# Expert routing of token pairs inside the output-projection stage, first expert block fixed and fetched early, residual written twice

## The reference, cut to what matters

```
mix = concat(groups) @ w_out
h   = LayerNorm(alpha * x + mix)
g_logits = h @ w_router_group + b          # 4 groups; the group with the largest logit is taken
e_logits = h @ w_router_expert + b         # 8 experts in that group; the top 2 are taken
gate = softmax(g_logits)[group] * softmax(top 2 logits)
moe  = sum over the 2 experts of gate * ((silu(h @ w1[e]) * (h @ w3[e])) @ w2[e])
out  = LayerNorm(alpha * h + moe)
```

## Time and profile before

| what | us |
|---|---|
| median of 3 runs (lowest, highest) | 2583.19 (2578.44, 2587.91) |
| the profiled execution, own time | 2585.68 |
| its span, first to last instruction | 2583.8 |
| third stage, from its first transfer to its last DVE instruction | 1304.89 to 1575.20 |
| fourth stage, to its last DVE instruction | to 1630.80 |
| first expert product | 1653.15 |
| fetches of expert weights (L1713), 2 MB each | 96 |

### The profile page before, as it was taken

The page is one execution under the profiler, slowest core; times in us unless marked ns, Lnnn a source line. Parts: engine busy times, 40 slices in busy tenths (PEclk is TensorE's granted clock), DMA queues, the critical chain, the costliest instruction groups (busy, mean ns, idle before and its releaser), DMA issues. The chain is left out here.

```text
span 2583.8 us, 42394 instructions
## 1 busy us (share of the span) xinstructions
PE 2292.1 (89%) x13288; PEld 1857.2 (72%) x13289; DVE 1595.6 (62%) x2749; ACT 1203.5 (47%) x1969; POOL 310.9 (12%) x223
## 2 busy tenths in 40 slices
PE   5999999897999999999959993599999999999950
PEld 5989998796666666666747882487877788888840
DVE  4444454555776767767745446577886765656538
ACT  4233334333665666656632220356765645446423
POOL 0000000000000000000001110013233322222315
PEclk9999999998999999999979996799999999999975
DMA  4001001121000000000043324599999978877825
GB/s 169 26 25 41 24 24 48 63 74 32 5 6 6 10 12 10 12 6 9 7 143 114 114 89 161 203 335 339 362 352 323 336 228 279 294 243 260 261 76 241
DMA packets 151085, 346.41 MB, mean 134 GB/s; under 512 B 25024, under 2 KB 37056, under 8 KB 150720
## 3 DMA queue, kind: packets, MB, share of 16 engines
q1 hardware_dynamic: 137888, 297.48, 31.7%
q0 software_dynamic: 13104, 47.72, 7.5%
HBM read 296.41 MB, written 57.67 MB: 137 GB/s over the span
## 5 line engine op out<-in xcount | busy, mean ns | idle before, releaser
L1862 DVE TENSOR_TENSOR w_raw<-w_raw,w_hi 128x4096 f32 (+1 forms) x96 | 424.2, 4419 | 142.0 <-ACT w_hi L1853 141.5
L1853 ACT CAST w_hi<-w_raw 128x4096 fp32r (+1 forms) x96 | 347.2, 3633 | 119.7 <-DMA w_raw<-in_w 109.0
L1802 PE MATMUL eH<-w_hi,xh 128*128 128x512 f32 x720 | 290.5, 404 | 15.5 <-DVE xl L1920 15.5
L1803 PE MATMUL eH<-w_hi,xl 128*128 128x512 f32 x720 | 286.7, 398 | 0.0
L943 PE MATMUL pS<-kT,qT 128*128 128x512 f32 (+3 forms) x640 | 260.2, 533 | 4.8 <-ACT pr L1032 4.4
L1040 ACT CAST prT_hi<-pT 128x512 fp32r<-128x512 f32 (+1 forms) x288 | 162.5, 564 | 197.9 <-PE pT L953 197.5
L1118 DVE TENSOR_TENSOR prT_lo<-pT,prT_hi 128x512 fp32r<-128x512 f32 (+1 forms) x288 | 189.4, 659 | 94.3 <-ACT prT_hi L1040 93.8
L1109 DVE TENSOR_REDUCE mx<-pS 128x1 f32<-128x512 f32 (+2 forms) x320 | 191.5, 608 | 15.3 <-PE pS L943 9.0
L1807 PE MATMUL eH<-w_raw,xh 128*128 x720 | 184.4, 398 | 5.5 <-DVE w_raw L1862 5.5
L943 PEld LDWEIGHTS pS<-kT,qT 128*128 128x128 f32 x640 | 111.2, 190 | 106.7 <-issue 61.9
L1802 PEld LDWEIGHTS eH<-w_hi,xh 128*128 128x128 f32 x720 | 136.6, 190 | 47.9 <-issue 15.3
(11 more groups left out here) (324 smaller groups left out, 4980.4 us busy)
## 6 DMA issues: line engine op xcount, KB each, us to landing
w_raw<-in_w SPq DMA_DIRECT2D x96, 2048.0 KB
xt<-in_x SPq DMA_DIRECT2D x16, 1024.0 KB, 5.0
xs<-in_x SPq DMA_DIRECT2D x8, 1024.0 KB, 5.0
scratch_h<-hp SPq DMA_DIRECT2D x16, 512.0 KB, 2.9
fz<-scratch_z SPq DMA_DIRECT2D x16, 512.0 KB, 10.8
out<-fz SPq DMA_DIRECT2D x16, 512.0 KB, 2.6
scratch_rT<-ot SPq DMA_DIRECT2D x8, 512.0 KB, 2.9
scratch_a<-a_out SPq DMA_DIRECT2D x64, 64.0 KB, 1.7
```

The source lines that it names most:

```text
L1802: pe.matmul(H[:], xh[:, k, :], w.hi[:, k, :], start=(k == 0), stop=False)
L1803: pe.matmul(H[:], xl[:, k, :], w.hi[:, k, :], start=False, stop=False)
L1853: nc.scalar.copy(w.hi[:], w.words(o).bitcast(F32)).then_inc(w.hi_ready, 1)
L1862: v.tensor_tensor(w.words(o), w.words(o).bitcast(F32), w.hi[:].bitcast(F32), ALU.subtract).then_inc(w.lo_ready, 1)
```

## The change

The picking of group and experts, the ranks and the one-hot rows for a pair of tiles are done in the third stage, two steps later: step m (from m = 2) does tiles 2(m - 2) and 2(m - 2) + 1. `choose` (21 DVE instructions, each waiting for the one before) stands behind `invert(m + 1)` and ahead of tile 0's L1423; one copy of the ranks stands behind tile 1's `split_r`; `ranked` and `spots` (14 instructions) stand at the end of the step, ahead of the next step's `split_a`. PE gets two small products ahead of tile 1's logits. Only the last four tiles are left for the fourth stage. A running count per expert (`carry`) replaces the scan over all tiles. Expert 0 always gets at least one block, so that block 0 belongs to expert 0 and its weights are fetched in the fourth stage without knowing the routing, with block 0's rows gathered there too. SP stores each tile of `h` a second time to `z` and the copy of `h` to `z` goes. The 32 products for tokens are separate from 32 products for gates, and block 0's rows depend on the first only. Router weights and constants are loaded in the third stage. In the fifth stage DVE splits block 0's rows before it splits w1.

```diff
+LATE = 4
+EARLY = (NT - LATE) // 2
+CHOOSE, PLACE = 21, 13
...
+def choose(v, go, t, s, pair, w):
...
+    go(v.tensor_tensor(t["gexp"][:, pair, :], G, bc(s["gmax"][:], NG), ALU.subtract))
+    go(v.tensor_tensor(s["geq"][:], G, bc(s["gmax"][:], NG), ALU.is_equal))
+    go(v.scalar_tensor_tensor(s["geq"][:], s["geq"][:], -64.0, row(R_LATE, NG), ALU.mult, ALU.add))
+    go(v.tensor_reduce(s["ix"][:], s["geq"][:], AX, ALU.min))
+
+    go(v.tensor_tensor(s["eq"][:], row(R_GROUP, NE), bc(s["ix"][:], NE), ALU.is_equal))
+    go(v.tensor_scalar(s["eq"][:], s["eq"][:], BIG, -BIG / 2, ALU.mult, ALU.add))
+    go(v.tensor_tensor(s["e1"][:], E, s["eq"][:], ALU.min))
+    for k, (src, m) in enumerate(((s["e1"], s["m1"]), (s["e2"], s["m2"]))):
+        go(v.tensor_reduce(m[:], src[:], AX, ALU.max))
+        go(v.tensor_tensor(s["eq"][:], src[:], bc(m[:], NE), ALU.is_equal))
+        go(v.scalar_tensor_tensor(s["eq"][:], s["eq"][:], -64.0, row(R_LATE, NE), ALU.mult, ALU.add))
+        go(v.tensor_reduce(s["ix"][:], s["eq"][:], AX, ALU.min))
+        go(v.tensor_tensor(t["oh"][:, k, pair, :], row(R_EXPERT, NE), bc(s["ix"][:], NE), ALU.is_equal))
+        if k == 0:
+            go(v.scalar_tensor_tensor(s["e2"][:], t["oh"][:, 0, pair, :], -BIG, s["e1"][:], ALU.mult, ALU.add))
+    go(v.tensor_tensor(s["both"][:], t["oh"][:, 0, pair, :], t["oh"][:, 1, pair, :], ALU.add))
+    go(v.tensor_tensor(t["de"][:, pair], s["m2"][:], s["m1"][:], ALU.subtract))
+
+
...
+    for i in range(w):
+        go(v.tensor_tensor(s["rk"][:, i], ranks[:, 0, i], t["carry"][:], ALU.add))
+        go(v.tensor_tensor(t["carry"][:], ranks[:, 1, i], t["carry"][:], ALU.add))
+
+
+def spots(v, go, t, s, pair, w):
...
+    go(v.tensor_scalar(s["qq"][:], s["sl"][:], 1.0 / P, -0.49609375, ALU.mult, ALU.add))
+    go(v.tensor_scalar(s["qq"][:], s["qq"][:], ROUND, None, ALU.add))
+    go(v.tensor_scalar(s["qq"][:], s["qq"][:], -ROUND, None, ALU.add))
+    go(v.scalar_tensor_tensor(s["sl"][:], s["qq"][:], -float(P), s["sl"][:], ALU.mult, ALU.add))
+    go(v.tensor_copy(t["q"][:, :, pair], s["qq"][:]))
+    go(v.tensor_tensor(t["at_row"][:, :, pair, :], t["rows"][:, R_BLOCK:R_BLOCK + P].unsqueeze(1).unsqueeze(1).broadcast_to([P, 2, w, P]),
+                       four(s["sl"][:]), ALU.is_equal))
+    for k in range(2):
+        go(v.tensor_tensor(t["at_tok"][:, k, pair, :], t["at_row"][:, k, pair, :], t["token"][:, pair].unsqueeze(2).broadcast_to([P, w, P]), ALU.mult))
+
+
+def route_scratch(sb, w):
...
+    def __init__(self, eng, sem, base):
+        self.eng, self.sem, self.base, self.n = eng, sem, base, 0
+
+    def __call__(self, ins):
+        self.n += 1
+        ins.then_inc(self.sem, 1)
+        self.eng.wait_ge(self.sem, self.base + self.n)
+
...
+                    if n == 3:
+                        for name, src in (("ga", d["mla_out_g"]), ("wr", d["w_router"].rearrange("(k p) n -> p k n", p=P)),
+                                          ("rb", d["b_router"].broadcast_to([P, NG + NE]))):
+                            sp.dma_start(t[name][:], src).then_inc(c_loaded, 16)
...
+                for name in ("rows", "before", "token"):
+                    sp.dma_start(t[name][:], d[name]).then_inc(r_consts, 16)
...
                         sp.dma_start(hd[m, i], hp[:, i]).then_inc(stored[i], 16)
+                        sp.dma_start(zd[m, i], hp[:, i]).then_inc(stored[i], 16)
...
+                def ranks(p):
+                    pe.wait_ge(routed, p * GROUP + CHOOSE - 1)
+                    both = rs["both"][:].rearrange("p n e -> p (n e)")
+                    pe.matmul(L[:, 64:64 + 2 * NE], t["before"][:], both, start=True, stop=True)
+                    pe.matmul(L[:, 64 + 2 * NE:64 + 4 * NE], t["ones"][:], both, start=True, stop=True)
...
+                    if pair is not None:
+                        ranks(pair)
...
+                    go = None
+                    if not isinstance(m, int) or m > 1:
+                        go = Chain(v, routed, (m - 2) * GROUP)
+                        choose(v, go, t, rs, pair_at(m - 2), 2)
...
+                    if go is not None:
+                        v.wait_ge(l_done, m * 2)
+                        go(v.tensor_copy(rs["ranks"][:], L[:, 64:64 + 4 * NE].rearrange("p (a n e) -> p a n e", a=2, n=2)))
                     if not first:
                         logged(m * 2 - 1)
                     turned(m * 2, 0)
-                v.wait_ge(c_loaded, 3 * 16)
+                    if go is not None:
+                        ranked(v, go, t, rs, rs["ranks"], 2)
+                        spots(v, go, t, rs, pair_at(m - 2), 2)
+                        assert go.n == GROUP
...
+                choose(v, go, t, s, late, LATE)
+                at["both"], at["de"] = go.n - 1, go.n
+
+                v.wait_ge(ranks, 1)
+                ranked(v, go, t, s, rk, LATE)
...
+                step(v.tensor_scalar(nblk[:], t["carry"][:], 1.0 / P, (P - 1.0) / P - 0.49609375, ALU.mult, ALU.add))
...
+                step(v.tensor_scalar(nblk[:, 0:1], nblk[:, 0:1], 1.0, None, ALU.max))
...
+                spots(v, go, t, s, late, LATE)
+
+                step(v.tensor_tensor(where[:], t["oh"][:], bbeg[:].unsqueeze(1).unsqueeze(1).broadcast_to([P, 2, NT, NE]), ALU.mult))
+                step(v.tensor_reduce(bb[:], where[:], AX, ALU.add))
+                step(v.tensor_tensor(bb[:], bb[:], t["q"][:], ALU.add))
+                for k in range(2):
+                    step(v.tensor_tensor(at_blk[:, k], rows[:, R_BLOCK:R_BLOCK + NBP].unsqueeze(1).broadcast_to([P, NT, NBP]),
+                                         bb[:, k].unsqueeze(2).broadcast_to([P, NT, NBP]), ALU.is_equal), f"at_blk{k}")
...
+                    step(v.tensor_tensor(at_gate[:, k], at_blk[:, k], scaled[:, k].unsqueeze(2).broadcast_to([P, NT, NBP]), ALU.mult), f"at_gate{k}")
+
+                v.wait_ge(tokens, 1)
+                v.tensor_scalar(t["idx"][:, 0:1], tk[:, 0:1], -1.0, 0.0, ALU.add, ALU.max).then_inc(idx_ready, 1)
...
+                v.wait_ge(gates, 1)
+                step(v.tensor_copy(t["share"][:], sh[:, 0:NBP]))
...
+                for k in range(2):
+                    pe.wait_ge(steps, at[f"at_blk{k}"])
+                    for n in range(NT):
+                        ins = pe.matmul(tk[:, 0:NBP], t["at_tok"][:, k, n], at_blk[:, k, n], start=(k == 0 and n == 0), stop=(k == 1 and n == NT - 1))
+                ins.then_inc(tokens, 1)
+                for k in range(2):
+                    pe.wait_ge(steps, at[f"at_gate{k}"])
+                    for n in range(NT):
+                        ins = pe.matmul(sh[:, 0:NBP], t["at_row"][:, k, n], at_gate[:, k, n], start=(k == 0 and n == 0), stop=(k == 1 and n == NT - 1))
+                ins.then_inc(gates, 1)
...
+            @block.gpsimd
+            def _(pool):
+                pool.wait_ge(idx_ready, 1)
+                Hold("add", t["cell"], t["hold_e"])(nc.gpsimd, 0)
+                nc.gpsimd.indirect_dma_start(out=t["xg"][:, 0], out_offset=None, in_=d["h"],
+                                             in_offset=bass.IndirectOffsetOnAxis(ap=t["idx"][:, 0:1], axis=0)).then_inc(gathered, 16)
...
-                for dst, src in ((rows, "rows"), (before, "before"), (restart, "restart_tiles"), (token, "token")):
-                    sp.dma_start(dst[:], d[src]).then_inc(loaded, 16)
...
-                for n in range(4):
-                    at_rows = slice(n * SEQ // 4, (n + 1) * SEQ // 4)
-                    sp.dma_start(d["z"][at_rows], d["h"][at_rows]).then_inc(copied, 16)
+                for name, k in (("w1", KT), ("w3", KT), ("w2", DE // P)):
+                    src = d[name][0, 0].rearrange("(k p) n -> p k n", p=P)
+                    with sp.Fori(0, 1) as zero:
+                        sp.dma_start(t[name + "_raw"][:, bass.ds(zero + k, k)].bitcast(F32), src).then_inc(t[name + "_loaded"], 16)
                 sp.dma_start(d["z"][SEQ:SEQ + P], d["h"][0:P]).then_inc(copied, 16)
-                sp.wait_ge(copied, 16 * 5)
...
                     if isinstance(b, int) and b == 0:
-                        for w in (w1, w3, w2):
-                            load(w, 0, 1, None)
                         return
...
-                index(0)
                 index(1)
+                x_part(0)
                 split_lo(v, w1, 0)
-                x_part(0)
```

More of the change, by code:

```diff
@@ new lines, in route_scratch @@
+def route_scratch(sb, w):
+    return {n: sb(f"r{w}_{n}", [P] + shape) for n, shape in (
+        ("gmax", [w]), ("geq", [w, NG]), ("ix", [w]), ("eq", [w, NE]), ("e1", [w, NE]), ("e2", [w, NE]), ("m1", [w]), ("m2", [w]), ("both", [w, NE]),
+        ("rk", [w, NE]), ("pr", [2, w, NE]), ("sl", [2, w]), ("qq", [2, w]), ("ranks", [2, w, NE]))}
+class Chain:
+    def __init__(self, eng, sem, base):
[4 more added lines that the diff above has]
+        self.eng.wait_ge(self.sem, self.base + self.n)
@@ L1203, in steps @@
             step(0, True, False)
-            with eng.Fori(1, STEPS - 1) as m:
```

(33 more changed lines are left out.)

186 lines of the change are left out of this document (80 added, 106 removed).

## The result

The changed kernel takes 2623.6 us (median of 4 runs, 2617.5 to 2624.94) against 2583.0 for the one before: 1.0139 times as long by the estimate over the runs, with a 95% interval of 1.012 to 1.0159 (the two medians alone give 1.0157). The forecast was 2606, so the sign was right and the size, +22.6, was a little over half of the +40.6 measured. The profiled execution spans 2622.1 us, 38.3 more than the earlier trace rows.

The account below looks back on a forecast made before the run. A chain through SP and DVE was taken to set the third stage's step, with PE following. Third stage +55.1, fourth -16.25, fifth -16.25 gave +22.6 us: 2583.2 becomes 2606, range 2587 to 2626.

Parts of the forecast that it names:

- the chain: Third stage: transfers through SP and DVE's work in sequence set the step's 29.6 us; PE is nearly full but follows.
- `choose` stands behind the wait: Third stage: `choose` follows DVE's 5.69 us wait for `ap`, so all its 5.1 us add to each middle step.
- the store adds on the `rts` side: Third stage: the second store delays the load behind it by 1.6 us, twice per step, for `ap` and for `rts`.
- steps 0 and 1 pay the stores alone: Third stage: step 0 has one load behind a second store, 1.6 us; step 1 has two, 3.2 us.
- the last step pays for the late `al` and the cold PE: Step 7, third stage: 4.6 us ahead of `al`, 2.7 for PE's halved clock, 0.5 for products and tail: +7.8 us.
- the fifth stage gains 16.25: Start of the fifth stage: first product at 6.1 us instead of 22.35, a gain of 16.25 us that stays.
- the constants at the start: Start of the third stage: constants arrive behind `b`, for which DVE waits, adding 1.0 us (0 to 3).
- Rival 1: Third stage: PE is the true bound, routing hides in DVE's idle time, growth some 9 us, total 2560; chance 0.13.
- the middle step: Third stage, steps 2 to 6: 29.5 + 5.1 + 2 x 1.6 = 37.8 us, 8.3 more each, 41.5 in all.
- `ranked` and `spots` were put at 4.6 and hidden: Third stage: 15 instructions, 4.6 us, ahead of the next `split_a`, hidden by the wait for `ap`.
- rival 3: Third stage: looped instructions pay 0.1 us for registers, `choose` 7.2, `spots` partly past its cover; total 2620; chance 0.14.
- the fourth stage: Fourth stage: 39.35 us instead of 55.6, gain 16.25, with PE's tokens at 29.5 us and gates hidden behind them.

Follow-up runs that it names:

- The wider products shown above: Changed kernel with the fourth stage's token products 130 columns wide instead of 65, the added columns never read: 2611.3 us.
- The one edit meant to test the lead: Changed kernel with the second expert's weight fetch no longer waiting for the cast of the first expert's: 2621.4 us.
- Three placements: Changed kernel with second stores behind the loads, `choose` ahead of `invert`, `ranked` and `spots` one step later: 2616.4, 2614.4, 2610.5 us alone; 2572.05 together.
- the two rearranged kernels with 65-column tokens: Changed kernel with `choose` ahead of `invert`, `ranked` and `spots` one step later; second stores behind the loads 2572.05 us, ahead of them 2583.9.

## Why the prediction was right and wrong

**Right: the chain.** That `choose` stands behind the wait and lies on the chain whole, that the store adds on the `rts` side, that steps 0 and 1 pay the stores alone, that the last step pays for the late `al` and the cold PE, and that the fifth stage gains 16.25: the ledger has them within 1.4 us each. The largest of these misses is the 1.0 us put down for the constants at the start. They cost nothing: tile 0's L1531 starts 40.2 us behind the stage's first transfer, and 40.3 before. Rival 1, that idle DVE time takes the routing up, did not come about; yet with the same work in other places and the stores behind the loads a step is 1 us longer than before, so it was the place and not the amount.

**A term mis-sized: the middle step, 8.3 for 9.4 (steps 3 to 6).** Three of its parts were off, in both directions. `choose` was put at 5.1 "since a repeated pair such as L1526 and L1527 shows 0.04 between them", but those stand outside a loop. In the loop it took 5.7, and written out the stretch shrank by 0.8. The second store was taken as 1.6 on either side, the transfer's row. Step 1 has the two sides without routing: their sum is the 3.2 counted, but by luck, for they are 2.1 and 1.1, and in the middle steps only the second is the store's. The Trainium skill (DMA: Bandwidth & Descriptors, Queues, rings and completion order) has each DMA engine take the descriptors of one ring in order. I had concluded from it that a load waits for the whole store ahead of it; the 2.1 and 1.1 for stores and loads of one size, and the half of the second that stays when the store stands behind, say that order alone does not set the price. And `ranked` and `spots` were put at 4.6 and hidden. The `al` behind them ends at 8.5 instead of 6.5 us, 0.9 of it because the first L1186 takes 1.10 us beside POOL's add and not 0.19. So this `al` holds ACT beyond the arrival of `ap`, and this excess takes the place of the store's delay on that side: 2.4 us where 1.6 was counted. By its mechanism that is rival 3 (0.1 us for registers, `spots` past its cover), which I gave 0.14. By the number it is not: the third stage grew by 59.2 us, my forecast had 55.1 and rival 3 some 69. That rival 3's total of 2620 lies nearest to 2623.6 is luck, and so in part is that 2623.6 lies inside a range whose upper end was built on rival 3: what filled it was the fourth stage and the expert blocks.

**The step that failed: the fourth stage, -16.25 for -8.4.** "PE's 32 products took 10.14 us for 64 passes; the same count gives tokens at 29.5. Gates follow and are hidden." The count was the same but not the width: 130 columns before, 65 now. With 65 the clock stayed at 0.50 for all 28 us, tokens took 13.9 and the gates 13.9 more, 4.24 of them uncovered. The wider products shown above bring the clock back and 8.5 us with it. I read the duration from the row and overlooked that its own clock, 0.50 and then 1.00, was part of it. The Trainium skill (TensorE: Matmul & The Clock Gate, Part 1) has the clock follow how busy PE is. This trace does not bear that out by itself: the profile shows no gap in PE from 1652.97 on, for 28 us, and the clock stays at 0.50. Why the width decides it is open; the runs show that it does.

**Not foreseen: the expert blocks, +5.6.** "PE is full behind it, so the gain stays" was true of the start only. Some 2 to 6 us are lost among the first 14 blocks in every kernel with the change. Rivals left: a smaller lead of the fetches, the place of `xg` and `y` in reused buffers, or the order of gathers and fetches. The one edit meant to test the lead did not move it.

## What to carry to other kernels

Idle time of an engine has a place. Put new work ahead of the wait that makes the idle time, not behind it, and check what stands in each wait already: here the same instructions cost 46.4 us over five steps in one order and about 6 in another. Three placements had to be right together; each alone gave a seventh to a quarter of the whole.

Before a duration of PE is carried over, compare width and granted clock of the row; here 64 passes with half the columns took 13.92 us instead of 10.14, because the clock stayed at 0.50. And a duration taken outside a loop over a register was too low for one inside.

## What the runs showed that was not expected

- Doubling the columns of the token products shortened them from 13.92 to 9.66 us, and the 65-column products behind them took 7.31 instead of 13.86 us: the clock, once risen, stayed up through products that had run at 0.50 throughout where they and others of their width came first.
- DVE's L1186, an add of two operands in SBUF, takes 0.19 us alone, and 1.10, 1.88 or 1.91 when it starts during POOL's add. It ends when POOL does: 1512.37 beside 1512.33, and 1470.77 beside 1470.72. In five traces (the changed kernel, `ranked` and `spots` one step later, the written-out steps, and the two rearranged kernels with 65-column tokens) all 27 long ones start during POOL's add and end 0.05 us behind it, and no short one starts during it. The Trainium skill (SBUF — State Buffer, SBUF: two separate sides) calls the port that both use an exclusive lock, held for a whole instruction, and names a DVE instruction with two SBUF inputs as one that needs it. The rows agree, though no run here took POOL's add away.
- Issued behind a load, a second store still cost that load about half of what it cost ahead of it: 0.54 of 1.16 us of DVE's wait for `rts` remained.
